# Meta-token products of the key and value projections: groups of four whole weight tiles in the first half of each pair, and groups of two tiles in halves, one weight tile later, in the second half

## The reference, cut to what matters

```python
    meta = jnp.broadcast_to(meta_tokens[None].astype(x.dtype), (B, N_META, D))
    h = jnp.concatenate([meta, x], axis=1)
    ...
        hn = _rmsnorm(h, attn_norm_w[l])
        proj = hn @ w_in[l]
        a_q, a_k, a_v, a_g, b_cq, b_ckv, b_kr, b_g = jnp.split(proj, list(splits), axis=-1)
    ...
        kvB = (_rmsnorm(b_ckv, mla_kv_norm_w[l]) @ w_ukv[l]).reshape(B, L_pad, B_HEADS, B_NOPE + B_V_DIM).transpose(0, 2, 1, 3)
```

## Time and profile before

| what | value |
|---|---|
| median of 3 runs | 1589.72 us (1586.89 to 4041.94) |
| the profiled execution, its own time | 1588.05 us |
| its span, first to last instruction | 1586.2 us |
| TensorE busy | 1573.2 us, 99% of the span |
| VectorE, ScalarE, GpSimd busy | 890.1, 812.7, 675.8 us |
| the key pair | 746.2 to 835.9 us of the span |
| the value pair | from 835.9 us |

### The profile page before, as it was taken

One profiled execution on the slowest core, in us unless ns is written; L12 is line 12 of the kernel. 1 busy time (PEld: TensorE's weight loads), 2 busy tenths in 40 slices (PEclk: granted clock), 3 DMA queues, 4 the chain that ended last, 5 costly groups with the idle time before them and its releaser, 6 DMA issues.

```text
span 1586.2 us, 22128 instructions
## 1 busy us (share of the span) xinstructions
PE 1573.2 (99%) x8143; PEld 1282.9 (81%) x8143; DVE 890.1 (56%) x1844; ACT 812.7 (51%) x1695; POOL 675.8 (43%) x569
## 2 busy tenths in 40 slices
PE   9999999999999999999999999999999999999998
PEld 7788888888888888897777688788878878888886
DVE  4257658674357776458554441323255454876675
ACT  5456766764334455454444366444466665344561
POOL 5553434436676404575110034544444426664022
PEclk9999999999999999999999999999999999999999
DMA  9454656656888978857999858554554325625762
GB/s 342 131 176 100 154 122 164 159 113 147 195 202 183 243 238 269 220 189 171 269 263 291 210 170 276 176 140 140 160 158 127 107 74 141 152 80 155 244 239 106
DMA packets 139383, 285.41 MB, mean 180 GB/s; under 512 B 11227, under 2 KB 17820, under 8 KB 138604
## 3 DMA queue, kind: packets, MB, share of 16 engines
q1 hardware_dynamic: 85660, 164.49, 31.4%
q0 software_dynamic: 31664, 81.70, 25.3%
q10 hardware_dynamic: 21952, 37.81, 7.5%
HBM read 259.01 MB, written 92.06 MB: 221 GB/s over the span
## 4 chain that ended last, share of the span: by engine, by line
PE 95%; DMA 2%; issue 1%; DVE 1%; ACT 1%; POOL 0%; POOLq 0%; ACTq 0%; DVEq 0%; SPq 0%
PE acc L740 15%; PE acc L742 15%; PE acc L741 15%; PE acc L756 4%; PE acc L758 4%; PE acc L757 4%; PE turn L1219 3%; PE acc L908 2%; PE acc L909 2%; PE acc L910 2%; PE sc L908 2%; PE turn L908 2%; PE sc L910 2%; PE sc L909 2%; PE turn L909 2%; PE turn L910 2%
## 5 line engine op out<-in xcount | busy, mean ns | idle before, releaser
L1970 POOL TENSOR_TENSOR w_lo<-w_raw,w_hi 128x512 fp32r<-128x512 f32 x341 | 510.3, 1505 | 648.4 <-ACT w_hi L1342 647.2
L1342 ACT ACTIVATE w_hi<-w_raw 128x512 fp32r<-128x512 f32 x565 | 354.2, 629 | 450.6 <-PE acc L742 178.9
L740 PE MATMUL acc<-w_hi,setA_hi 128*128 128x512 f32 (+1 forms) x820 | 330.6, 403 | 0.5 <-ACT stage L1356 0.4
L742 PE MATMUL acc<-w_hi,setA_lo 128*128 128x512 f32 (+1 forms) x820 | 316.0, 385 | 0.0
L741 PE MATMUL acc<-w_lo,setA_hi 128*128 128x512 f32 (+1 forms) x820 | 314.7, 384 | 0.0
L2395 DVE TENSOR_TENSOR w_lo<-w_raw,w_hi 128x512 fp32r<-128x512 f32 x224 | 155.7, 701 | 135.0 <-ACT w_hi L1342 134.4
L742 PEld LDWEIGHTS acc<-w_hi,setA_lo 128*128 128x128 f32 x820 | 153.9, 188 | 31.6
L740 PEld LDWEIGHTS acc<-w_hi,setA_hi 128*128 128x128 f32 x820 | 154.4, 188 | 26.4 <-issue 2.1
L741 PEld LDWEIGHTS acc<-w_lo,setA_hi 128*128 128x128 f32 x820 | 154.7, 189 | 24.1
L756 PE MATMUL acc<-setA_hi,w_hi 128*128 128x512 f32 x256 | 101.9, 398 | 0.0
L758 PE MATMUL acc<-setA_lo,w_hi 128*128 128x512 f32 x256 | 99.9, 390 | 0.0
(11 more groups left out here) (553 smaller groups left out, 3209.2 us busy)
## 6 DMA issues: line engine op xcount, KB each, us to landing
w_raw<-in_swa_w_in SPq DMA_DIRECT2D x35, 1024.0 KB, 7.2
w_raw<-in_w_in SPq DMA_DIRECT2D x32, 1024.0 KB, 5.4
w_raw<-sum_out SPq DMA_DIRECT2D x64, 256.0 KB, 4.7
sum_k<-in_w_in POOLq DMA_DIRECT2D x24, 512.0 KB, 6.7
sum_out<-in_swa_w_out POOLq DMA_DIRECT2D x24, 512.0 KB, 8.1
sum_v<-in_w_in POOLq DMA_DIRECT2D x24, 512.0 KB, 8.6
w_raw<-in_w_in SPq DMA_DIRECT2D x48, 256.0 KB, 5.7
sum_out<-in_w_out POOLq DMA_DIRECT2D x24, 512.0 KB, 6.8
```

The source lines that it names most:

```text
L740: mm(acc[t][:, 0:cols], hi[:, kc, rows], wh, start=(k == 0), stop=False)
L742: last = mm(acc[t][:, 0:cols], lo[:, kc, rows], wh, start=False, stop=(k == K - 1))
L1342: nc.scalar.activation(w_at(f)[0], raw_of(f), ACT.Copy).then_inc(done, 1)
L1970: nc.gpsimd.tensor_tensor(lo, raw_of(f), hi.bitcast(F32), ALU.subtract).then_inc(s_lo, 1)
```

## The change

In the first half the groups of four tiles (`meta_fours(c, M)`, M = 0 to 3) take the place of the eight groups of two. Each of the four matmuls has a whole tile of 512 columns, and each quarter of the bank now holds all 512 columns of one tile. In the second half the groups are as before but stand one tile later. The table says at which product a group stands and whose raw tiles it takes.

| before | after |
|---|---|
| product 0: tiles 0, 1; product 1: tiles 3, 4 | product 1: tiles 0, 1, 3, 4 |
| product 4: tiles 6, 7; product 7: tiles 9, 10 | product 5: tiles 6, 7, 9, 10 |
| product 10: tiles 12, 13; product 13: tiles 15, 16 | product 11: tiles 12, 13, 15, 16 |
| product 16: tiles 18, 19; product 19: tiles 21, 22 | product 17: tiles 18, 19, 21, 22 |
| T = 8 to 15: product 3T - 2 | T = 8 to 15: product 3T - 1 |

`meta_use` follows: tiles 0, 1, 3, 4 are free for SP after product 1, then 6, 7, 9, 10 after product 5, and so on. Since every quarter now holds all columns, ScalarE copies one quarter of 512 columns in one instruction, and VectorE adds three quarters, one after the other, where it added two halves.

```diff
-                    meta_use[B[c] + p] = B[c] + max(3 * T - 2, 0) + 1 + 4
+                    meta_use[B[c] + p] = B[c] + (max(6 * (T // 2) - 1, 1) if T < 8 else 3 * T - 1) + 1 + 4
...
+            def meta_fours(c, M):
+
+                of = (*meta_tiles(c, 2 * M), *meta_tiles(c, 2 * M + 1))
+                for p, _ in of:
+                    slot, i, target = raw_at[B[c] + p]
+                    pe.wait_ge(s_tile[4 * slot + i], target)
+                for n, (p, unit) in enumerate(of):
+                    mm(acc[2][2 * META * n:2 * META * (n + 1)], meta_full[:, unit:unit + 2].rearrange("p a b -> p (a b)"),
+                       raw_of(B[c] + p), start=(M == 0), stop=False)
...
-                                if i == 0 and m == 0:
-                                    if c == "k":
-                                        pe.wait_ge(s_evac, 4 * E[14] + 4 + 3)
-                                    else:
-                                        pe.wait_ge(s_mevac, 3)
-                                    meta_products(c, 0)
...
-                                if i == 0:
-                                    meta_products(c, m + 1)
+                                if i == 0 and m == 0:
+                                    if c == "k":
+                                        pe.wait_ge(s_evac, 4 * E[14] + 4 + 3)
+                                    else:
+                                        pe.wait_ge(s_mevac, 3)
+                                    meta_fours(c, 0)
...
+                                if i == 0 and m in (1, 3, 5):
+                                    meta_fours(c, m // 2 + 1)
+                                if i == 0 and m == 7:
+                                    meta_products(c, 8)
...
-                                if i == 0 and m < 7:
-                                    meta_products(c, m + 9)
...
+                                if i == 0 and m < 7:
+                                    meta_products(c, m + 9)
...
                 if m in (1, 2):
-                    for half in range(2):
-                        part = total[:, half * CW // 2:(half + 1) * CW // 2]
-                        last = V.tensor_tensor(part, meta_quarter(bank, 0, half), part, ALU.add)
-                    last.then_inc(s_mevac, 1)
+                    for n in (0, 2):
+                        after(dve, V.tensor_tensor(total, bank[2 * META * n:2 * META * (n + 1)], total, ALU.add))
+                    V.tensor_tensor(total, bank[6 * META:8 * META], total, ALU.add).then_inc(s_mevac, 1)
```

More of the change, by code:

```diff
@@ L1013, in meta_products @@
                                   meta_full[:, unit:unit + 2].rearrange("p a b -> p (a b)"),
-                                  raw_of(B[c] + p)[:, half * CW // 2:(half + 1) * CW // 2], start=(T == 0), stop=(T == 15))
+                                  raw_of(B[c] + p)[:, half * CW // 2:(half + 1) * CW // 2], start=False, stop=(T == 15))
                 if T == 15:
@@ L1364, in evacuate_meta @@
                     act.wait_ge(s_mstage, m)
-                if m in (1, 2):
-                    for half in range(2):
-                        last = nc.scalar.activation(sum_of(m)[:, half * CW // 2:(half + 1) * CW // 2], meta_quarter(bank, 1, half), ACT.Copy)
-                    last.then_inc(s_mtmp, 1)
-                    return
                 nc.scalar.activation(sum_of(m)[:, 0:cols], bank[32:32 + rows, 0:cols], ACT.Copy).then_inc(s_mtmp, 1)
```

## The result

The changed kernel took 1591.24 us (median of 18 runs, 1588.62 to 1595.61) where the kernel before took 1587.94 in the same comparison. The ratio is 1.0024, 95% interval 1.0016 to 1.0031: 2.5 to 4.9 us slower, far inside 2%. 1593.6 had been predicted, with 1585.2 to 1598.0 as the range. The profiled execution took 1591.03 us, with a span of 1589.2.

A forecast was written before the change was run, and what follows sets the result against it. TensorE's own queue was taken to bound the kernel (95% of the last chain). Terms -2.9 + 0 + 0 + 4.7 + 1.0 + 0.4 + 2.4 = +5.6 us on 1588.05 gave 1593.6 us, range 1585.2 to 1598.

The forecast's parts named there:

- The groups, -2.9: First halves of both pairs: four groups of 1.20 us replace eight of 0.78; -2.9 us (-6.2 to +0.5).
- the rival of +3.4: First-half groups: four different tiles don't stream beside each other; +3.4 us on any case; no chance given.
- The second half, 0: Second-half groups: release and need both move one product later, old waits of 1.4 us stay; 0 (-1.4 to +1.4).
- Adding up, 0: VectorE's three additions before product 55: at most 2.04 us, one microsecond of cover left; 0.
- The wait before the second key group, +4.7: Key pair, product 5: TensorE waits for tile 10, loaded late beside GpSimd's copies; +4.7 us.
- the estimate by bytes: Key pair: tile 10's landing reckoned from bytes through SP's queue, 757.7, or 759.7 with 0.2 MB more.
- my second rival: Key pair loads as fast as tile 10 before (5.3 us), waits 1.5 and 0.4, clock whole; 1587.1 us, chance 0.18.
- The value pair, +1.0: Value pair's second group: the same 3.8 us for loads, wait of 0 to 2.4 us, taken as +1.0.
- later groups, +0.4: Groups at products 11 and 17: loads late perhaps once where GpSimd's copies meet them; +0.4 us (0 to 3).
- The clock, +2.4: After the key pair's stop of over 4 us: one fall of the granted clock; +2.4 us (0 to 5).
- my first rival: Key pair: the stop comes but the clock stays whole; 1591.2 us, chance 0.27.

The follow-up runs named there:

- second_only: Kernel before with only the second half's groups of two one weight tile later, tiles freed one product later; 1586.87 us, ratio 0.9991.
- fours_in_k: Changed kernel with groups of four in the key pair alone; value pair's first half as before, second half later in both pairs; 1592.92 us, ratio 1.0023.
- late_release: Kernel before, groups where they were, but tiles of every other step held one product longer, as the changed kernel holds them; 1590.44 us, ratio 1.0014.
- The deliberate stops: Kernel before with TensorE waiting ahead of key-pair product 43 for 13 or 30 GpSimd memsets; 1591.21 us (1.0018) and 1596.24 us (1.0053).
- at_0_copies_early: Changed kernel with the first group of four at product 0 in both pairs and GpSimd's four 512 KB copies issued earlier; 1584.75 us, ratio 0.9979.

## Why the prediction was right, step by step

The sign and the mechanism were right, and the time lies in the range. The place was right in the profiled execution; other executions waited elsewhere. The forecast was +5.6 us; the median gave +3.3, the ratio +3.8, and the two pairs of the profiled execution +6.0.

- **The groups, -2.9.** A group of four took 1.20 us, as worked out from the step, the old group and the float32 matmuls. Four tiles stream beside each other as well as the halves of two; the rival of +3.4 is out.
- **The second half, 0.** This term was mis-sized, within its bounds: I kept the old waits of 1.4 us, and `second_only` gained 1.4 (0.2 to 2.9). I had held one product later for both release and need to be neutral. In the traces the waits at these groups shrink from 2.0 to 0.7 us in the mean, which fits the gain; why a load then comes in time more often no run shows.
- **Adding up, 0.** VectorE's timeline at the end of the key pair, which answers the earlier trace rows:

```profile
834.89 1.39 DVE L2578 TENSOR_TENSOR tmp_early<-acc,tmp_early 32x512 f32<-32x512 f32 x2
836.32 0.69 DVE L2579 TENSOR_TENSOR tmp_early<-acc,tmp_early 32x512 f32<-32x512 f32 x1
836.94 1.87 DVE L2402 TENSOR_TENSOR w_lo<-w_raw,w_hi 128x512 fp32r<-128x512 f32 x3
```

  TensorE at product 55:

```profile
838.52 0.39 PE L908 MATMUL turn<-w_hi,setA_hi 128*128 128x512 f32 x1
```

  The three additions take 2.05 us where 2.04 was the bound. The low part of tile 55, the first of the three in the last row, is made by about 837.6, and product 55 starts at 838.52: the one microsecond of cover is there, to a tenth.
- **The wait before the second key group, +4.7.** It was 4.72 us, for tile 10, whose load took 8.4 us; 0.48 and 0.71 MB had gone through SP's queue from 747 to 757, more than the 0.79 of its three tiles, as the estimate by bytes had assumed. That the second decimal fits is luck: the same key pair in `fours_in_k` waited 4.4 us in three pieces, only 0.4 of it here. There SP's loads got ahead of the copies and tile 10 took 4.2 us, which is what my second rival asked for; that the loss then comes at later groups the forecast had only as 0.4 us, and the rival not at all. What the prediction hadn't said is that the hold alone is dear (`late_release`, +2.2), not only the earlier need.
  The Trainium skill, page "DMA: Bandwidth & Descriptors", section "Anatomy of one DMA", gives a fixed 2.0 us and bytes over 436 GB/s for one transfer (fitted on GpSimd's path), an estimate of 2.6 us for 256 KB. The fastest load here took 2.6; beside GpSimd's copies they took 8.4 to 12.2, so for this wait the rule is a floor and not a price.
- **The value pair, +1.0, and later groups, +0.4.** Measured 1.5 in two waits and 1.1 at product 17, where the copies' followers meet the loads. The first was too small by a third, the second by two thirds.
- **The clock, +2.4.** In the profiled execution products 5 to 7 show its price: from the second group's start at 757.15 to product 8 at 764.56 there are 7.41 us, where the first group and its rest took 747.49 - 745.69 = 1.80 and two products take 2.73: 2.9 us. The deliberate stops show that a stop is enough for it.
  The Trainium skill's page "TensorE: Matmul & The Clock Gate", section "Why this matters for your kernels", has this rule, that an idle gap between bursts of matmuls brings the half clock back, and the traces of the stops agree with it: 0.50 for 3.4 us after 2.34 us, 0.50 for 6.8 after 4.72. Stops of 2.25 to 2.93 us, shorter than the gaps that it warns of, were enough here; stops of 2.00 and 2.22 us had no fall.

The forecast was 1.8 us above what the ratio gives. Taken from the ratios, the changed kernel gave 2.9 for groups and 1.4 for the second half and lost 3.8 in all: its waits and falls cost 8.1 us in the mean, for 4.7 + 1.0 + 0.4 + 2.4 = 8.5 predicted. What made the forecast miss is thus mostly the term for the second half, which had been set to 0 (its 1.4 is known to within 0.2 to 2.9). The median equals the time of my first rival, in which the clock doesn't fall; the traces show that it does, so this agreement is a coincidence of sums.

With both remedies 1.0 us of the 4.3 that the groups and the second half give is still lost, by its one profile in the wait at the fourth key group.

## What to carry to other kernels

An instruction that takes more tiles at once has two prices beside its own time: it holds the first of them longer and asks for the last of them earlier, and both are taken from the time of the same loads. Work that slack out first, in us from the release of a place to the need of what comes into it, and set it beside the slowest loads of the trace, not the median. Where it falls short, move the transfers that crowd these loads before giving up the merge: here that and a release one product earlier turned a loss of 3.8 us into a gain of 3.3. And where one execution decides where a wait falls, judge by many runs, and by the sum of the waits rather than by the group that shows it.

## What the runs showed of the hardware

- The granted clock fell to 0.50 in mid-program after eight stops of TensorE, in eight executions (2.25, 2.27, 2.34, 2.37, 2.93, 3.08, 4.72 and 5.09 us), for 3.4 us each time and for 6.8 after the one of 4.72. After stops of 2.22, 2.00 and 1.98 us it stayed at 1.00. The fall began between 0.6 us before TensorE's next matmul and 1.7 us after it.
- Loads of 256 KB by SP took 3.3 to 4.5 us with few others about (tiles 8 to 10 in `at_0_copies_early`) and 8.4 to 12.2 beside four copies of 512 KB by GpSimd, while the DMA engines moved 285 GB/s (tiles 10 to 13 in the changed kernel). Little more than half a microsecond made the difference: tile 10 took 4.2 us where it was issued 0.58 us ahead of the first copy, and 8.4 where it was issued 0.05 us behind it.
- A float32 group in four column groups costs 0.78 us with 256 columns and 1.20 with 512: 0.42 for doubling the columns. By these two, an estimate of 0.36 doesn't depend on them.
